# A hybrid attention, delta-rule and mixture-of-experts layer: GpSimd's sums in quarters, a copy moved on VectorE, a split load and a reordered DMA queue

## The reference

```
h = rms_norm(x);  proj = h @ w_in                     # 1024 x 5640, one combined projection
y_a = diff_attention(dq, dk, dv)                      # 4 heads, two softmaxes each, P1 - lam * P2
y_b = gated_delta_net(gq, gk, gv, beta, decay, gate)  # conv + silu, chunked delta rule, norm * silu(gate)
merged = sigmoid(m_gate_a) * (y_a @ w_branch_attn) + sigmoid(m_gate_b) * (y_b @ w_branch_gdn)
x = x + merged @ w_out
x = x + hier_moe(rms_norm(x))                         # 32 experts in 4 groups, top 2, hidden 256
y = rms_norm(x)
```

## Time and profile before

| what | value |
|---|---|
| median of three runs | 465.39 us |
| time of the profiled execution | 467.6 us |
| its span, first to last instruction | 465.5 us |
| TensorE matmul busy | 427.6 us (92%) |
| TensorE weight loads busy | 341.1 us (73%) |
| VectorE busy | 225.9 us (49%) |
| ScalarE busy | 124.7 us (27%) |
| GpSimd busy | 53.2 us (11%) |
| mean granted TensorE clock | 0.967 |
| DMA | 136.92 MB, mean 294 GB/s |

### The profile page before, as it was taken

How to read it: one execution, slowest core, us unless ns; L and a number is a source line. 1 busy time by engine, 2 the same in 40 slices (tenths; PEclk the granted TensorE clock), 3 DMA queues, 4 the chain that set the end, 5 groups by cost and what they waited for, 6 DMA issues and landing times.

```text
span 465.5 us, 10695 instructions
## 1 busy us (share of the span) xinstructions
PE 427.6 (92%) x4503; PEld 341.1 (73%) x4503; DVE 225.9 (49%) x573; ACT 124.7 (27%) x326; POOL 53.2 (11%) x46
## 2 busy tenths in 40 slices
PE   8999999999999996999899899999999977779784
PEld 7885698874889986988788788677686745537451
DVE  3367677995663696212222546353444613332224
ACT  5002523001400452410012434232232402322144
POOL 4010500000863561000000000000000000000001
PEclk9999999999999997999999899999999988998798
DMA  8969725407504314099996799999999999999992
GB/s 309 409 216 340 284 66 193 157 31 215 188 4 179 112 71 180 1 358 419 402 372 256 292 356 415 417 420 421 424 421 421 422 422 422 422 422 419 420 369 99
DMA packets 38180, 136.92 MB, mean 294 GB/s; under 512 B 8576, under 2 KB 9920, under 8 KB 26240
## 3 DMA queue, kind: packets, MB, share of 16 engines
q1 hardware_dynamic: 33792, 135.22, 73.7%
q10 hardware_dynamic: 4352, 1.21, 1.2%
HBM read 134.59 MB, written 1.84 MB: 293 GB/s over the span
## 4 chain that ended last, share of the span: by engine, by line
PE 71%; DMA 23%; issue 2%; DVE 2%; ACT 1%; POOLq 0%; ACTq 0%; DVEq 0%
PE ps L988 21%; DMA arena<-in_moe_w_up 13%; PE ps L1032 10%; PE ps L1436 9%; PE ps L1300 6%; DMA ring<-in_moe_w_up 6%; PE ps L1489 3%; PE ps L1479 3%; DMA arena<-in_w_out 3%; PE ps L1284 3%; PE ps L1395 3%; PE ps L1444 1%; PE ps L1047 1%; PE ps L1197 1%; DMA cst_in<-in_norm_ffn_gain 1%
## 5 line engine op out<-in xcount | busy, mean ns | idle before, releaser
L988 PE MATMUL ps<-arena 128*128 128x256 f32 (+1 forms) x384 | 98.6, 416 | 0.0
L988 PEld LDWEIGHTS ps<-arena 128*128 128x128 f32 x384 | 72.2, 190 | 22.3 <-issue 13.8
L1436 PE MATMUL ps<-arena 128*32 128x128 f32 x1040 | 40.2, 296 | 10.9 <-DMA arena<-in_moe_w_up 10.4
L1436 PEld LDWEIGHTS ps<-arena 128*32 128x32 f32 x1040 | 30.9, 115 | 18.0 <-DMA arena<-in_moe_w_up 7.7
L785 ACT ACTIVATE gains<-ps 32x256 f32<-32x256 f32 x62 | 23.4, 377 | 55.3 <-PE ps L1479 55.0
L2183 DVE TENSOR_TENSOR masks<-ps,masks 128x64 f32<-128x64 f32 x32 | 7.2, 224 | 55.2 <-ACT masks L766 55.0
L551 POOL TENSOR_SCALAR ring<-ring,small 128x512 f32<-128x512 f32 x1 | 1.6, 1567 | 281.8 <-DVE small L2137 281.8
L2199 DVE COPY arena<-ps 32x256 f32<-32x256 f32 x62 | 25.8, 416 | 11.2 <-PE ps L1479 10.2
L1300 PE MATMUL ps<-arena 128*128 128x256 f32 x128 | 29.3, 384 | 1.2 <-DMA arena<-in_w_out 1.2
L1436 PE MATMUL ps<-ring,arena 128*32 128x128 f32 x768 | 26.5, 277 | 3.4 <-DMA ring<-in_moe_w_up 3.3
L1284 PE MATMUL ps<-arena 128*128 128x256 f32 x128 | 28.0, 379 | 0.0
(11 more groups left out here) (324 smaller groups left out, 605.9 us busy)
## 6 DMA issues: line engine op xcount, KB each, us to landing
arena<-in_moe_w_down SPq DMA_DIRECT2D x19, 1024.0 KB, 26.0
arena<-in_w_in SPq DMA_DIRECT2D x9, 2048.0 KB, 8.3
arena<-in_moe_w_gate SPq DMA_DIRECT2D x16, 1024.0 KB, 22.5
arena<-in_moe_w_up SPq DMA_DIRECT2D x16, 1024.0 KB, 24.5
ring<-in_moe_w_gate SPq DMA_DIRECT2D x12, 1024.0 KB, 20.7
ring<-in_moe_w_up SPq DMA_DIRECT2D x12, 1024.0 KB, 20.7
ring<-in_moe_w_down SPq DMA_DIRECT2D x12, 1024.0 KB, 22.1
arena<-in_w_out SPq DMA_DIRECT2D x2, 2048.0 KB, 13.0
```

The costliest lines, as they stand in the source:

```text
L988: last = pe.matmul(out, lhs, rhs, start=(k == 0 and (i > 0 or part % 2 == 0)), stop=(k == KD - 1), skip_group_check=(i == 0))
L1436: last = pe.matmul(c.ps[ROWS * q:ROWS * (q + 1), i % 2, 0:P], c.Hg[:, k, ROWS * i:ROWS * (i + 1)], w[:, :, start:start + 127:2], start=(k ...
```

## The change

It has five parts.

1. GpSimd makes each of the sixteen sums in four instructions over 128x256 elements instead of one over 128x1024; the counts of `combined` follow.
2. The load of chunk ma0 is split into two DMAs of 1 MB each (first half: A11 and A21, counted by `first_loaded`). P1 of ma0 waits for the first half only; P2 and GpSimd wait for both.
3. TensorE's order changes around ma0: each product there is placed one step earlier against the side work, so that P1 of ma0 stands ahead of `scores(0)`, and P1 of ma1 ahead of `turn_probs(0)`.
4. VectorE: `combine(0)` goes behind the take-out of TT6 (L1990), and `add_product("mb0", "C11")` and `probs_turned(1)` go ahead of the eight scalings of L2029.
5. SyncE: the first half of w_out is loaded ahead of expert 3.

```diff
 def combined(name, form):
-    return 4 + len(COMBINED) * SEVEN.index(name) + COMBINED.index(form) + 1
+    return 4 + 4 * (len(COMBINED) * SEVEN.index(name) + COMBINED.index(form) + 1)
...
+        if i == CI["ma0"]:
+            k0 = KD // 2
+            sp.dma_start(dst[:, 0:k0, :], w_in[:, 0:k0, col:col + n]).then_inc(s["first_loaded"], 16)
         sp.dma_start(dst[:, k0:, :], w_in[:, k0:, col:col + n]).then_inc(s[f"stage_loaded{i % 2}"], 16)
...
     load_expert(OWN - 1)
-    sp.wait_ge(s["ybT_ready"], 1)
-    sp.wait_ge(s["ya_ready"], 1)
-    load_expert(3)
     for j in range(2):
...
         if j == 0:
+            sp.wait_ge(s["ybT_ready"], 1)
+            sp.wait_ge(s["ya_ready"], 1)
+            load_expert(3)
             load_expert(SLOTS - 1)
...
+        def combine(out, one, other, op):
+            for k in range(4):
+                pool.tensor_tensor(form[out][:, k, :], one[:, k, :], other[:, k, :], op).then_inc(s["forms_combined"], 1)
         pool.wait_ge(s[f"stage_loaded{i % 2}"], 16 * (i // 2 + 1))
+        if name == "ma0":
+            pool.wait_ge(s["first_loaded"], 32)
         free("P5")
-        pool.tensor_tensor(form["S1"], w["A21"], w["A22"], ALU.add).then_inc(s["forms_combined"], 1)
+        combine("S1", w["A21"], w["A22"], ALU.add)
...
-            if product == "P1":
+            if product == "P1" and name == "ma0":
+                pe.wait_ge(s["first_loaded"], 32)
+            elif product == "P1" or product == "P2":
                 pe.wait_ge(s[f"stage_loaded{i % 2}"], 16 * (i // 2 + 1))
...
+    products("ma0", "P1")
     scores(0)
-    products("ma0", "P1", "P2")
+    products("ma0", "P2", "P5")
...
-    products("ma0", "P5", "P6")
+    products("ma0", "P6", "P4")
...
-    products("ma0", "P4")
+    products("ma0", "P3")
...
-    products("ma0", "P3")
+    products("ma0", "P7")
     solve(0)
-    products("ma0", "P7")
+    products("ma1", "P1")
     turn_probs(0)
     first_outputs_and_state()
-    products("ma1", "P1", "P2")
+    products("ma1", "P2")
...
-    combine(0)
-
     v.tensor_scalar(c.TT[halves(0), :, halves(1)], ...)
...
+    combine(0)
     add_product("ma0", "C12")
     solved(0)
...
     v.wait_ge(s["gate_ready"], 2)
+    add_product("mb0", "C11")
+    probs_turned(1)
     for i in range(8):
         b = blk(c.flat["TT"], i)
         last = v.scalar_tensor_tensor(out=b, in0=b, scalar=col(c.rb, i), in1=blk(c.flat["gate"], i), op0=ALU.mult, op1=ALU.mult)
...
-    add_product("mb0", "C11")
-    probs_turned(1)
     add_product("mb0", "C12")
```

More of the change, by code:

```diff
@@ L536, in free @@
                 pool.wait_ge(s["proj_ready"], product_done(SEVEN[n_ - 1], product))
+        def combine(out, one, other, op):
+            for k in range(4):
+                pool.tensor_tensor(form[out][:, k, :], one[:, k, :], other[:, k, :], op).then_inc(s["forms_combined"], 1)
         pool.wait_ge(s[f"stage_loaded{i % 2}"], 16 * (i // 2 + 1))
+        if name == "ma0":
+            pool.wait_ge(s["first_loaded"], 32)
         free("P5")
-        pool.tensor_tensor(form["S1"], w["A21"], w["A22"], ALU.add).then_inc(s["forms_combined"], 1)
+        combine("S1", w["A21"], w["A22"], ALU.add)
         pool.wait_ge(s["forms_combined"], combined(name, "S1"))
         free("P6")
-        pool.tensor_tensor(form["S2"], form["S1"], w["A11"], ALU.subtract).then_inc(s["forms_combined"], 1)
+        combine("S2", form["S1"], w["A11"], ALU.subtract)
         pool.wait_ge(s["forms_combined"], combined(name, "S2"))
         free("P3")
-        pool.tensor_tensor(form["S4"], w["A12"], form["S2"], ALU.subtract).then_inc(s["forms_combined"], 1)
+        combine("S4", w["A12"], form["S2"], ALU.subtract)
         free("P7")
-        pool.tensor_tensor(form["S3"], w["A11"], w["A21"], ALU.subtract).then_inc(s["forms_combined"], 1)
+        combine("S3", w["A11"], w["A21"], ALU.subtract)
     pool.wait_ge(s["r2_ready"], 1)
```

## The result

The changed kernel takes 459.13 us, the median of four runs (458.74 to 460.23), against 465.31 us for the kernel before in the same measurement. The ratio is 0.986, interval 0.983 to 0.989. That is 6.2 us faster; forecast were 11.2, and the time lies 0.9 us above the range. The profiled execution has a span of 458.5 us, where before had 465.5; that distance of 7.0 us is of one execution each, and the one of before was a long one (467.6 us).

The account below looks back on a forecast made before the run. TensorE's path ahead of 257.7 us was taken to set the end by starting the expert weight stream. Gains of 5.7 + 3.1 + 1.3 + 1.1 = 11.2 us from 465.4 gave 454.2 us, range 452.5 to 458.2.

Parts of the forecast that it names:

- the stall: TensorE's idle time ahead of `weigh_values(1)`, at 173.44 us: all 5.7 us go with the probabilities' copy ahead of the scalings.
- the clock behind it: TensorE at low clock in `weigh_values(1)` and P1, P2 of mb1: returns to full clock, 3.1 us less.
- w_out: Ahead of the output product (`mix`): loading the first half ahead of expert 3 removes the wait, gain 1.1 us.
- the order around ma0: Gaps ahead of `scores(0)` and `solve(0)` close, `combine(0)` ends later: net gain 1.3 us, bounds 2.2 and -1.9.
- come in pairs at each end of a GpSimd instruction: VectorE beside GpSimd's quarters: two operations per 0.8 us, so eight scalings take 3.2 us instead of 9.95, `combine(0)` 4.0.
- second rival: One VectorE operation per GpSimd boundary; `solve` and first output late, 3.2 us lost: 457.4 us, 458.4 with P6's wait. Chance 0.12.
- the upper bound: Order around ma0: with `combine(0)` undisturbed at 2.4 us, the gain is 2.2 us.
- its lower bound: The eight scalings ahead of `weigh_values(1)`'s successors: 2.19 us with GpSimd at rest, ending at 173.2 us.
- the third (the clock): A new or shifted wait leaves TensorE at 1.2 GHz as long as now; 3.1 us stay: 457.3 us. Chance 0.08.
- late `yb_ready`: Scalings behind the copy end at 173.2 to 176.4 us, TensorE wants `yb_ready` at 177.6: no wait.
- P1 of ma0 in the gap ahead of `scores(0)`: P1 of ma0 fills the 0.94 us that TensorE idles for VectorE's take-out of Y5.
- the split load in time for it: P1 of ma0's half of the load is there by 115.4 us; P1 starts at 116.7.

Follow-up runs that it names:

- eighths: The changed kernel with two GpSimd instructions of 128x128 in place of each quarter: median 455.5 us, ratio to the kernel before 0.978.
- whole sums: The changed kernel with GpSimd's sums whole again (128x1024), all else of the change kept: median 457.6 us, ratio to the kernel before 0.982.
- the yielding run: The changed kernel, quarters kept, with GpSimd waiting for the end of `combine(0)` ahead of ma1's S2: 455.0 us, ratio 0.976; measured again, 453.99 us, 0.975.
- the repeated profile of the changed kernel: The changed kernel with no further edit, measured again on one chip beside the version in which GpSimd yields: 459.97 us, ratio 0.987.
- idle work: The changed kernel with 14 products that nobody reads put on TensorE ahead of `turn_probs(0)`: median 457.8 us, ratio to the kernel before 0.981.
- quarters alone: The kernel before with GpSimd's sums in quarters and nothing else: median 462.55 us against 465.44, ratio 0.993.
- the last pair: The changed kernel and the one where GpSimd waits for the end of `combine(0)`, measured together on one chip: 459.97 and 453.99 us.

## Why the prediction was wrong

The bound was right, and so were three of its four terms. Against the forecast's 5.7 for the stall, 3.1 for the clock behind it and 1.1 for w_out, the profile after shows 5.71, 3.1 and 1.2 (the waits and slow rows that are no longer there). The sum failed in the third term, the order around ma0: forecast +1.3 us, measured -4.7. It held two mistakes: how long `combine(0)` would be held, and that the idle time from it would leave the clock as it was. The first output began at 142.69 us instead of before's 138.77, with one product of 1.79 us more done: -2.1 (that includes 0.65 us by which `turn_probs(0)` was slow). It and the product behind it then took 1.89, 1.71 and 2.56 us instead of 0.89, 0.89 and 1.79 at the low clock: -2.6. Together 5.71 + 3.1 - 4.7 + 1.2 = 5.3 us, and `mix` starts 227.17 - 221.83 = 5.34 us earlier.

The step that failed is the reading that VectorE's operations "come in pairs at each end of a GpSimd instruction". I took it from one pair and the count "eight scalings took four of GpSimd's instructions". Instruction by instruction, the kernel before shows this (queries of short stretches of VectorE's timeline; a stretch of x2 or x3 holds several):

```profile
167.63 1.74 DVE L2029 SCALAR_TENSOR_TENSOR arena<-arena,small 128x128 f32<-128x128 f32 x1
...
169.30 2.52 DVE L2029 SCALAR_TENSOR_TENSOR arena<-arena,small 128x128 f32<-128x128 f32 x1
...
171.74 2.71 DVE L2029 SCALAR_TENSOR_TENSOR arena<-arena,small 128x128 f32<-128x128 f32 x2
...
174.37 2.42 DVE L2029 SCALAR_TENSOR_TENSOR arena<-arena,small 128x128 f32<-128x128 f32 x1
...
176.72 0.86 DVE L2029 SCALAR_TENSOR_TENSOR arena<-arena,small 128x128 f32<-128x128 f32 x3
```

With the 2.44 us at 172.00 of the earlier trace rows, the starts are 167.63, 169.30, 171.74, 172.00, 174.37 and then three from 176.72. Only one extra operation slips in, at 171.74, between the second and the third sum. Four operations were held, one by each of the four sums, one slipped in, and the last three ran after GpSimd had finished. An average over a run that outlives the contention had made one per boundary look like two. The Trainium skill, SBUF — State Buffer, "Who interferes with whom", has it as an exclusive lock that is held for the whole instruction; its strict reading was the nearer one, and the 812 ns a scaling beside quarters and 3.94 us for eight beside eighths agree with it.

What GpSimd costs a run of VectorE operations is therefore one instruction for each operation, until the operations or GpSimd's instructions run out. Quarters shorten each hold and make four times as many holds possible. That is why they help where one tiny operation stands between engines (the maxima), and at the scalings in the old order (9.95 us against four whole sums, 6.21 against eight quarters), win little at the scalings in the new order (6.44 against 6.08), and hurt in `combine(0)`. There, with whole sums, GpSimd was waiting for TensorE part of the time and one operation was held for long; with quarters nine operations met a quarter each.

Both signs that the forecast had set for its second rival came: the first output at 142.69 us (142.5) and the eight scalings in 6.08 (6.4). TensorE could have been 1.8 us ahead there, as the yielding run shows, and not the 2.2 of the upper bound. One small slip in the forecast changed nothing: scalings that take the 2.19 us of its lower bound end at 172.2, not at 173.2, which belongs to 3.2 us.

By the forecast's rivals, the second (one operation per boundary) came true, and the third (the clock) came with it as its consequence. I had priced them apart, at 457.4 and 457.3. Together they are 454.2 + 3.2 + 3.1 = 460.5, against 459.1 measured. They were not independent: the new idle time was over 3 us, and I had only asked whether 0.7 us would slow the clock.

What the sum did not have is on the other side. The whole span gained 7.0 us and the end of `mix` only 5.6, so 1.4 us came behind `mix`. In the profile before, TensorE's clock fell during the routing:

```profile
262.00:264.00 2.00, 1.00 (x11) 1.00 (x12) 1.77 (x12) 1.97 (x4) 0.00 (x0) 0.94 1.03 434
264.00:266.00 2.00, 2.00 (x17) 1.32 (x20) 1.74 (x9) 0.16 (x2) 0.00 (x0) 0.50 1.00 422
266.00:268.00 2.00, 2.00 (x21) 1.19 (x11) 0.01 (x1) 1.03 (x2) 0.00 (x0) 0.71 0.96 331
```

and in the first profile of the changed kernel it did not (256 to 264 us in the windows above), where the first reload of a used slot was issued 12.0 us after the end of `mix` instead of 13.1. But that is no gain of the change: in the repeated profile of the changed kernel the clock fell there too, and the reload came after 13.4 us. Nor does it explain the 1.4 us. In the five of the twelve profiles in which the clock fell in the routing, the time from the end of `mix` to the end of the span was 205.9 to 207.8 us, in the seven others 206.4 to 206.8. So no run ties the 1.4 us to the change, and that the measured time is only 0.9 us above the range is in this part luck.

Right were also: the copy ahead of the scalings with no late `yb_ready` behind it, P1 of ma0 in the gap ahead of `scores(0)`, the split load in time for it, no wait for GpSimd's sums, and the second half of w_out in time.

What stays open: why the clock falls in the routing in some executions (before, idle work, quarters alone, both of the last pair) and not in the seven others, with the same idle time of 1.4 us ahead. It is not the kernel, since the changed kernel and the yielding one have a profile of either kind. Why the same gap cost 3.2 us in one profile of the changed kernel and 2.0 in the other is open too. The runs of the yielding kernel lie in two groups, spans of 452.1 and 454.2 to 454.9 us in the first measurement, 451.4 to 451.5 and 452.9 to 453.5 in the last. The routing's clock alone does not divide them, for it fell (0.67) in the profiled run of 451.4; the slower ones have no trace. Parts 2 and 3 of the change, the split load and P1 of ma0 ahead of `scores(0)`, were seen in the profile but not undone in a run of their own.

## What to carry to other kernels

When two engines take turns at a lock, count holds one by one in the trace, never as a mean over a run that ends in free time; splitting the other engine's work into smaller instructions bounds a single hold and does not shorten the total (here 2.78 us for a sum in quarters, 2.35 whole). If the other engine has slack, let it wait for the short critical chain instead: here that is one semaphore wait and was worth 6 us. And price a new idle time on TensorE together with the clock that it may cost, not as a separate case.

## What the runs showed of the hardware

- While GpSimd's sums ran back to back, VectorE's scalings and scalar_tensor_tensor (128x128, inputs in SBUF) got in one for each GpSimd instruction: 2.4 us beside sums of 1024 elements, 0.76 beside 256, 0.49 beside 128. The same operations with GpSimd at rest take 0.27 to 0.35 us. Now and then one slips in unheld between two GpSimd instructions (0.34 us at 171.74 in the kernel before).
- Size does not protect: a tensor_scalar of 128x4 took 2.07 us beside a whole sum and 0.17 with quarters in the yielding run. Not every operation is held: the reciprocal of 128x8 took 0.20 us at 167.40 in the middle of a whole sum, and the copy out of PSUM 1.23 us beside GpSimd's quarters and 1.21 in the earlier trace rows with GpSimd at rest.
- Quarters of a sum cost 2.78 us where the whole costs 2.35.
- The granted clock fell after 5.7, 3.2, 3.0 and 2.5 us without work on TensorE (means of 0.50, 0.57, 0.60 and 0.59 in the stretch behind), and stayed at 1.00 after 1.97 and 1.16 us. Ahead of the routing 1.4 us without work were followed by the low clock in five profiles and not in seven. The loss behind the first four gaps was 3.1, 3.2, 2.0 and about 1.9 us; some 0.2 of each is the first group behind a wait, which is longer at full clock too (2.02 us instead of 1.79 for sixteen rows in the run with quarters alone).
